# TensorE takes both halves' high products of a weight unit before both halves' low ones

## The chip, the cores and the metric

The kernel runs on one core of a Trainium2 chip. The metric is the device time of one execution in microseconds (us), as the median of several. The engines are TensorE (PE in the rows, its weight loads PEld), VectorE (DVE), ScalarE (ACT), GpSimd (POOL) and SyncE (SP, which here issues the DMAs of the weights). Each runs its own list of instructions in order, and they wait for each other by semaphores.

## The reference

Two transformer blocks work on 256 tokens of width 1024, in float32. The first is an attention layer with compressed, selected and windowed keys. The second has two layers: a mixer (stick-breaking attention beside a short convolution), then a dense feed-forward part in layer 0 and a mixture of experts in layer 1, and a gated projection. Cut to what matters:

```python
for i in range(DEPTH_2):
    ...                                   # h = h + mixed @ w_o[i]
    f = rmsnorm(h, ffn_norm_g[i])
    if i % 2 == 0:
        h = h + swiglu(f, dense_w1[j], dense_w3[j], dense_w2[j])
    else:                                 # top 2 of 8 experts, 1024 -> 3584 -> 1024
        h = h + moe_swiglu(f, router_w[j], moe_w1[j], moe_w3[j], moe_w2[j])
    gate = jax.nn.sigmoid(rmsnorm(h, ple_norm_g[i]) @ ple_gate_w[i])
    h = h + gate * (p[i] @ ple_proj_w[i])
```

## The kernel before

**Three products for one.** A float32 matrix product is made from products of the shorter type fp32r: each operand is split into a high part (the value rounded) and a low part (the rest), and PE adds up high x high and low x high (activations times `wh`, L1471 and L1472) and high x low (`wl`, L1476).

**Weight units.** All weights come in units of 128 partitions x 2048 columns (1 MB; some are smaller): as a rule four k tiles of 512 output columns. SyncE loads unit u into one of 6 buffers `raw` (L466) when DVE has finished with unit u-6 (`low_done`). ACT copies it half by half (two k tiles each) to `whi`, one of 3 buffers (`SPL`, L549), and DVE subtracts to get `wlo` (L892). ACT waits, half by half, for `half_used`: PE has finished with that half of unit u-3. It tells DVE and PE by `high_done`, DVE tells PE and SyncE by `low_done`. Where each of the two stands in its own list with its splits is written out by hand: `split_to(v)` makes all halves up to unit v, and between such calls stand the other steps of the stage.

**Products.** `products` (L1461) does one unit: for each half it waits for `high_done`, takes the high products of its k tiles for all output tiles, waits for `low_done`, takes the low ones, and gives the half back with `half_used`. A callback `middle` runs before the second half. `block` (L1482) does the units of one output block; in the first block after a norm its `middle` is `turn_rows(norm, 1)`, which transposes the second half of the token rows (L1527; the rows of the trace show the helper's line, L1454). ACT scales and copies these to `xh` (L565), DVE makes `xl` (L903), and PE waits for that (`xl_done`, L1492) before the second unit. That happens in four blocks: the first of each mixer and the first of each gated projection. Two more calls have a `middle`: the last unit of the dense part (L1745) and the first after the attention (L1696). `unit_T` (L1698) does units with the weights as the stationary operand (L1716, L1717, L1723), with the same order written out; it stands for the second half of each mixer's input and for most of the dense part. `z_half` (L1584) calls `products` for one half at a time.

**The expert rounds.** 8 rounds (L1937), one for each expert, of 42 units; one output tile of 128 gathered tokens, so that a unit is 12 products. First 7 hidden blocks of 4 units (gate, up), with `turn_hidden` between; ACT makes the activation (L735) and copies the turned hidden block (`mTh`, L726), DVE multiplies (`ht`, L1158) and takes the low part (`mTl`, L1149). Then 14 units of the second weight. After six of them PE gathers the next round's tokens (`gather(1)`, L1928 and L1929), for which it waits for `pick` (L1395): DVE makes it after its subtractions for the two units that come behind the gather (`split_to(ub + 4 * NFB + 5 + AHEAD)`, L1166). ACT and DVE then split the gathered tokens (`xgh`, `xgl`). At the end ACT and DVE split the expert's result (`yh` L864, `yl` L1431), and PE scatters it back to the tokens (L1955, L1956). DVE makes `yl` after its subtractions for the first two units of the next round.

Of the kernel before, what the change touches and what calls it, by code (L numbers as in the profile page):

```python
# [108 lines left out]
def build(nc, t, out):  # L109
# [25 lines left out]
    with ExitStack() as ctx:  # L135
# [1313 lines left out]
        def _(pe):  # L1449
# [6 lines left out]
            def split_view(u, nk, n):  # L1456
                s = u % SPL
                return (whi[:, s, 0:nk * n].rearrange("p (k n) -> p k n", k=nk),
                        wlo[:, s, 0:nk * n].rearrange("p (k n) -> p k n", k=nk))

            def products(u, nk, n, hi, lo, k0, outs, first, last, middle=None, halves=(0, 1)):  # L1461

                wh, wl = split_view(u, nk, n)
                for half in halves:
                    if half and middle:
                        middle()
                    ks = range(half * nk // 2, (half + 1) * nk // 2)
                    pe.wait_ge(high_done, g.at(high_done, 2 * u + half + 1))
                    for k in ks:
                        for T, o in enumerate(outs):  # L1470
                            mm(o, hi(k0 + k, T), wh[:, k, :], start=first and k == 0, stop=False)  # L1471
                            mm(o, lo(k0 + k, T), wh[:, k, :], start=False, stop=False)  # L1472
                    pe.wait_ge(low_done, g.at(low_done, 2 * u + half + 1))
                    for k in ks:
                        for T, o in enumerate(outs):
                            ins = mm(o, hi(k0 + k, T), wl[:, k, :], start=False, stop=last and k == nk - 1)  # L1476
                    ins.then_inc(half_used, 1)
# [4 lines left out]
            def block(u, b, hi, lo, kt=KD, n=NB, nt=NT, units=None, norm=None, between=None):  # L1482


                bank = pair(b)
                outs = [ps[:, bank + T, 0:n] for T in range(nt)]
                start_block(b)
                ku = units or KU
                nu = -(-kt // ku)
                for i in range(nu):  # L1490
                    if norm is not None:
                        pe.wait_ge(xl_done, 2 * norm + i + 1)  # L1492
                    if i and between:
                        between()
                    products(u + i, min(ku, kt - i * ku), n, hi, lo, i * ku, outs, i == 0, i == nu - 1,
                             (lambda: turn_rows(norm, 1)) if norm and i == 0 else None)
# [87 lines left out]
            def z_half(i):  # L1584

                if i % 4 == 0 and i:

                    pe.wait_ge(z_done, i // 4)
                u = i // 2
                products(U["z"] + u, KU, NB, *X, (u % 2) * KU, [ps[:, T, :] for T in range(NT)], u % 2 == 0,  # L1590
                         u % 2 == 1, halves=(i % 2,))
# [94 lines left out]
            for i in range(2):  # L1686
                b = B["nsa_out"] + i
                outs = [ps[:, pair(b) + T, :] for T in range(NT)]
                if i == 0:

                    pe.wait_ge(o_evac, 9)
                for k in range(2):
                    if i == 0:
                        pe.wait_ge(yl_done, k + 1)
                    products(U["nsa_out"] + 2 * i + k, KU, NB, *X, k * KU, outs, k == 0, k == 1,
                             (lambda: turn_y(1)) if i == 0 and k == 0 else None)  # L1696
# [397 lines left out]
```

## Time and profile before

| | us |
|---|---|
| median of 3 runs | 1921.33 (1921.16 to 1925.42) |
| the profiled execution | 1927.16 |
| its span, first to last instruction | 1925.3 |
| PE busy | 1838.6 (95%) |
| DVE busy | 1395.7 (72%) |
| ACT busy | 1220.0 (63%) |
| mean granted clock of PE | 0.974 |

All times below are counted from the span's start. In a row of the timeline stand the start, the length, the engine, the line, the operation, what it writes and reads, how many like it follow each other, and, where the engine stood idle before, for how long and what ended that. Products overlap in PE's pipeline, so the distance from one start to the next is the pace, not the length. A wait for several semaphores is put down to the one that came last by the profile; "issue" is a wait for nothing that it shows.

### The profile page before, as it was taken

What the parts mean: (1) busy time and instruction counts of PE and PEld (TensorE: products, weight loads), DVE (VectorE), ACT (ScalarE), POOL (GpSimd) and SP (SyncE); (2) the same over time, 40 slices, a digit from 0 to 9 for tenths busy, and PEclk for the clock granted to TensorE, in tenths of its full rate; (3) what the DMA queues carried; (4) which work ended last, traced back from release to release, by engine and by line L of the source; (5) the groups of instructions that cost most, each with busy time, mean ns of one, the idle gap of its engine ahead of it and who ended that gap; (6) DMA issues with size and microseconds to landing.
All of it is one profiled execution on the core that took longest, in us unless ns stands there. A gap on an engine that the chain in (4) does not pass through costs nothing.

```text
span 1925.3 us, 26803 instructions
## 1 busy us (share of the span) xinstructions
PE 1838.6 (95%) x9562; PEld 1546.2 (80%) x9562; DVE 1395.7 (72%) x1653; ACT 1220.0 (63%) x1536; POOL 5.9 (0%) x13
## 2 busy tenths in 40 slices
PE   8999979989999989879999999999999999999997
PEld 7877758979998779768878878788788787887885
DVE  4456755746664466458899898898998898989884
ACT  5545544644444455548687777786877777768773
POOL 0000000000000000000000000000000000000000
PEclk9889989999999999879999999999999999999999
DMA  9743223425445344219989899899898998998980
GB/s 321 248 165 109 74 102 131 154 100 190 177 190 202 111 175 176 93 67 339 369 319 362 317 364 364 310 367 355 325 361 319 352 360 325 358 345 343 357 323 23
DMA packets 68336, 483.32 MB, mean 251 GB/s; under 512 B 7610, under 2 KB 7738, under 8 KB 10928
## 3 DMA queue, kind: packets, MB, share of 16 engines
q1 hardware_dynamic: 66480, 475.26, 64.9%
q0 software_dynamic: 1792, 7.18, 1.8%
q8 instruction: 44, 0.72, 0.2%
q14 instruction: 20, 0.16, 0.0%
HBM read 478.22 MB, written 4.19 MB: 251 GB/s over the span
## 4 chain that ended last, share of the span: by engine, by line
PE 80%; DVE 8%; ACT 6%; issue 5%; DMA 0%; ACTq 0%; DVEq 0%; POOLq 0%
PE ps L1471 20%; PE ps L1472 19%; PE ps L1476 19%; DVE wlo L892 4%; PE ps L1716 4%; PE ps L1723 4%; PE ps L1717 4%; PE ps L1454 3%; ACT whi L549 2%; PE ps L1928 1%; PE ps L1929 1%; ACT xgh L846 1%; DVE sg L1015 1%; ACT sg L672 1%; PE ps L1819 1%
## 5 line engine op out<-in xcount | busy, mean ns | idle before, releaser
L892 DVE TENSOR_TENSOR wlo<-raw,whi 128x1024 fp32r<-128x1024 f32 x906 | 1044.1, 1212 | 171.8 <-ACT whi L549 171.3
L549 ACT ACTIVATE whi<-raw 128x1024 fp32r<-128x1024 f32 x906 | 904.2, 1055 | 154.6 <-PE ps L1476 127.4
L1471 PE MATMUL ps<-whi,xgh 128*128 128x512 f32 x896 | 360.2, 402 | 4.6 <-ACT whi L549 4.6
L1472 PE MATMUL ps<-whi,xgl 128*128 128x512 f32 x896 | 355.0, 396 | 0.0
L1476 PE MATMUL ps<-wlo,xgh 128*128 128x512 f32 x896 | 282.2, 396 | 0.0
L1471 PE MATMUL ps<-whi,xh 128*128 128x512 f32 (+1 forms) x448 | 186.9, 418 | 21.9 <-issue 9.9
L1471 PEld LDWEIGHTS ps<-whi,xgh 128*128 128x128 f32 x896 | 168.9, 188 | 43.1 <-ACT whi L549 4.8
L1476 PEld LDWEIGHTS ps<-wlo,xgh 128*128 128x128 f32 x896 | 168.9, 188 | 40.8
L1472 PEld LDWEIGHTS ps<-whi,xgl 128*128 128x128 f32 x896 | 169.2, 189 | 37.8
L1472 PE MATMUL ps<-whi,xl 128*128 128x512 f32 (+1 forms) x448 | 181.3, 406 | 0.0
L1471 PE MATMUL ps<-whi,mTh 128*128 128x512 f32 x448 | 178.3, 398 | 0.0
L1472 PE MATMUL ps<-whi,mTl 128*128 128x512 f32 x448 | 177.1, 395 | 0.0
L1716 PE MATMUL ps<-xh,whi 128*128 128x256 f32 x640 | 157.9, 284 | 0.5 <-DVE xl L903 0.5
L1717 PE MATMUL ps<-xl,whi 128*128 128x256 f32 x640 | 157.0, 283 | 0.0
L1476 PE MATMUL ps<-wlo,mTh 128*128 128x512 f32 x448 | 140.9, 395 | 0.0
L1471 PEld LDWEIGHTS ps<-whi,xh 128*128 128x128 f32 x448 | 90.3, 202 | 43.5 <-issue 20.6
L1476 PE MATMUL ps<-wlo,xh 128*128 128x512 f32 (+1 forms) x448 | 123.8, 401 | 0.0
L1716 PEld LDWEIGHTS ps<-xh,whi 128*128 128x128 f32 x640 | 122.7, 192 | 1.0 <-DVE xl L903 0.7
L1717 PEld LDWEIGHTS ps<-xl,whi 128*128 128x128 f32 x640 | 122.8, 192 | 0.1
L1472 PEld LDWEIGHTS ps<-whi,xl 128*128 128x128 f32 x448 | 90.3, 202 | 17.6 <-issue 0.2
L1476 PEld LDWEIGHTS ps<-wlo,xh 128*128 128x128 f32 x448 | 87.8, 199 | 18.9
L1476 PEld LDWEIGHTS ps<-wlo,mTh 128*128 128x128 f32 x448 | 84.2, 188 | 20.4
(288 smaller groups left out, 1902.5 us busy)
## 6 DMA issues: line engine op xcount, KB each, us to landing
raw<-in_w_moe_dram SPq DMA_DIRECT2D x336, 1024.0 KB, 6.7
raw<-in_w_fixed_dram SPq DMA_DIRECT2D x112, 1024.0 KB, 4.9
bias_scratch<-revb POOLq DMA_DIRECT2D x1, 3072.0 KB, 39.2
bias<-bias_scratch POOLq DMA_DIRECT2D x1, 2048.0 KB, 18.2
raw<-in_w_fixed_dram SPq DMA_DIRECT2D x4, 512.0 KB, 4.2
tok<-in_xt_dram SPq DMA_DIRECT2D x2, 512.0 KB, 4.5
h<-in_x_dram SPq DMA_DIRECT2D x1, 1024.0 KB, 13.6
out_dram<-h SPq DMA_DIRECT2D x2, 512.0 KB, 2.8
```

What stands on the lines that cost most here:

```text
L549: AC(whi[:, v % SPL, c], raw[:, v % RAW, c], ACT.Copy).then_inc(high_done, 1)
L672: ins = AC(sg[:, i % 2, r, 0:nk], sg[:, i % 2, r, 0:nk], ACT.Exp, scale=SC, bias=ast_[:, i, 1, r:r + 1], accum_out=ast_[:, i, 2, r:r + 1])
L846: ins = AC(xgh[:, j, :], ps[:, 6 + j // 4, (j % 4) * P:(j % 4 + 1) * P], ACT.Copy, scale=gains[:, 5, j:j + 1])
L892: V.tensor_tensor(wlo[:, v % SPL, c], raw[:, v % RAW, c], whi[:, v % SPL, c].bitcast(F32), ALU.subtract).then_inc(low_done, 1)
L1015: ins = V.tensor_tensor_reduce(sg[:, i % 2, r, 0:nk], ps[:, bank, (r // 2) * S:(r // 2) * S + nk], bias[:, hh, S - nk:S], 1.0, MASKED, ALU ...
L1454: return nc.tensor.transpose(dst, src, ident if idn is None else idn)
L1471: mm(o, hi(k0 + k, T), wh[:, k, :], start=first and k == 0, stop=False)
L1472: mm(o, lo(k0 + k, T), wh[:, k, :], start=False, stop=False)
L1476: ins = mm(o, hi(k0 + k, T), wl[:, k, :], start=False, stop=last and k == nk - 1)
L1716: mm(o, w_, xh[:, kk, :], start=kk == 0 and c % 2 == 0, stop=False, skip_group_check=True)
L1717: mm(o, w_, xl[:, kk, :], start=False, stop=False, skip_group_check=True)
L1723: ins = mm(o, wl[:, k, c * P:(c + 1) * P], xh[:, kk, :], start=False, stop=kk == KD - 1, skip_group_check=True)
```

## The change

In `products` the loop over the halves is cut in two: first, for each half, the wait for its high part, and its high products (`middle` still comes ahead of the second half); then, for each half, the wait for its low part, its low products and the signal `half_used`. With two halves the order is high 0, (`middle`), high 1, low 0, low 1 in place of high 0, low 0, (`middle`), high 1, low 1. A call for one half does what it did. `unit_T` isn't touched.

```diff
                 for half in halves:
                     if half and middle:
                         middle()
-                    ks = range(half * nk // 2, (half + 1) * nk // 2)
                     pe.wait_ge(high_done, g.at(high_done, 2 * u + half + 1))
-                    for k in ks:
+                    for k in range(half * nk // 2, (half + 1) * nk // 2):
                         for T, o in enumerate(outs):
                             mm(o, hi(k0 + k, T), wh[:, k, :], start=first and k == 0, stop=False)
                             mm(o, lo(k0 + k, T), wh[:, k, :], start=False, stop=False)
+                for half in halves:
                     pe.wait_ge(low_done, g.at(low_done, 2 * u + half + 1))
-                    for k in ks:
+                    for k in range(half * nk // 2, (half + 1) * nk // 2):
                         for T, o in enumerate(outs):
                             ins = mm(o, hi(k0 + k, T), wl[:, k, :], start=False, stop=last and k == nk - 1)
                     ins.then_inc(half_used, 1)
```

## Rows read from the trace of the kernel before

**Rows 1.** The page, part 4: the chain that ended last, by engine.

```profile
PE 80%; DVE 8%; ACT 6%; issue 5%; DMA 0%; ACTq 0%; DVEq 0%; POOLq 0%
```

**Rows 2.** Busy us, expert rounds: length; PE, PEld, DVE, ACT, POOL; clock, DMA share, GB/s.

```profile
857.00:1880.00 1023.00, 1015.58 (x4589) 821.29 (x4590) 890.37 (x909) 774.30 (x887) 0.00 (x0) 1.00 0.89 341
```

**Rows 3.** Waits of PE and PEld, 860 to 1880: total us, times, longest.

```profile
PE ps L1955 <- DVE yl L1431: 6.2, 8, 0.8
...
PEld ps L1955 <- DVE yl L1431: 9.7, 8, 1.2
PEld ps L1928 <- issue: 4.4, 8, 0.6
```

**Rows 4.** Line L892 (DVE's subtractions), whole span: who waited for it (us, times).

```profile
  PEld ps L1723: 0.4, 2
```

**Rows 5.** Timeline of PE: the unit before the last one ahead of the gather.

```profile
1207.61 0.40 PE L1471 MATMUL ps<-whi,mTh 128*128 128x512 f32 x1
...
1208.54 0.63 PE L1476 MATMUL ps<-wlo,mTh 128*128 128x512 f32 x2
...
1210.40 0.40 PE L1471 MATMUL ps<-whi,mTh 128*128 128x512 f32 x1
```

**Rows 6.** Timeline of ACT and DVE in the loop over the hidden blocks.

```profile
1179.72 0.69 DVE L1149 TENSOR_TENSOR mTl<-ps,mTh 128x512 fp32r<-128x512 f32 x1 [0.91 <-ACT mTh L726]
...
1185.81 1.22 DVE L892 TENSOR_TENSOR wlo<-raw,whi 128x1024 fp32r<-128x1024 f32 x1
...
1185.95 1.06 ACT L549 ACTIVATE whi<-raw 128x1024 fp32r<-128x1024 f32 x1 [0.34 <-PE ps L1476]
```

**Rows 7.** Timeline of ACT and DVE ahead of the gather.

```profile
1202.71 4.84 ACT L549 ACTIVATE whi<-raw 128x1024 fp32r<-128x1024 f32 x5
...
1209.20 1.06 ACT L549 ACTIVATE whi<-raw 128x1024 fp32r<-128x1024 f32 x1 [0.34 <-PE ps L1476]
...
1203.79 9.17 DVE L892 TENSOR_TENSOR wlo<-raw,whi 128x1024 fp32r<-128x1024 f32 x8 [0.26 <-ACT whi L549]
1212.88 0.48 DVE L1395 TENSOR_SCALAR pick<-con,slot 128x128 fp32r<-128x128 f32 x2
```

**Rows 8.** Timeline of PE: into the gather, and the first product behind it.

```profile
1212.74 0.63 PE L1476 MATMUL ps<-wlo,mTh 128*128 128x512 f32 x2
1213.49 0.32 PE L1928 MATMUL ps<-pick,xnh 128*128 128x128 f32 x1
...
1217.11 0.45 PE L1471 MATMUL ps<-whi,mTh 128*128 128x512 f32 x1
```

**Rows 9.** Timeline of ACT, DVE and PE at the end of a round.

```profile
1235.56 1.06 ACT L549 ACTIVATE whi<-raw 128x1024 fp32r<-128x1024 f32 x1 [0.34 <-PE ps L1476]
...
1237.49 2.34 DVE L892 TENSOR_TENSOR wlo<-raw,whi 128x1024 fp32r<-128x1024 f32 x2
1239.76 1.31 DVE L1431 TENSOR_TENSOR yl<-ps,yh 128x512 fp32r<-128x512 f32 x2
...
1240.49 0.51 PE L1955 MATMUL ps<-yh,pickT 128*128 128x512 f32 x1 [0.77 <-DVE yl L1431]
```

**Rows 10.** First block of the first gated projection, timeline; then L1471's wait, 0 to 1925.

```profile
664.26 1.07 PE L1476 MATMUL ps<-wlo,xh 128*128 128x512 f32 x4
...
666.25 1.57 ACT L565 ACTIVATE xh<-ps,con 128x256 fp32r<-128x256 f32 x4 [6.20 <-PE ps L1454]
...
667.89 1.07 PE L1476 MATMUL ps<-wlo,xh 128*128 128x512 f32 x4
...
669.56 0.50 PE L1471 MATMUL ps<-whi,xh 128*128 128x512 f32 x1 [0.60 <-DVE xl L903]
...
PE ps L1471 <- DVE xl L903: 6.0, 5, 3.5
```

**Rows 11.** Busy us by stretch, as rows 2: around a wait, and at the last stage's start.

```profile
405.00:415.00 10.00, 8.43 (x42) 6.77 (x41) 5.33 (x8) 3.46 (x6) 0.00 (x0) 1.00 0.12 36
...
1886.00:1892.50 6.50, 4.91 (x12) 3.85 (x13) 1.35 (x4) 0.00 (x0) 0.00 (x0) 0.50 0.00 0
```

## The prediction

> **What bounds the kernel now.** I read the chain that ended last first: TensorE (PE) is 80% of it, most of it weight products [rows 1]. Then the busy times by stage: the expert rounds, from 857 to 1880 us, are over half of the span, and in them PE is busy for 1015.6 of 1023 us at full clock, with VectorE (DVE) at 87% and ScalarE (ACT) at 76% [rows 2]. The waits of that stretch name only two places where PE stands still, each once in every one of the 8 rounds: before the scatter (L1955, 6.2 us of PE idle in all), and before the gather (L1928, where only the weight loads' row shows it, 4.4 us) [rows 3]. No low half of a weight unit ever kept a product of L1476 waiting; the two waits for DVE's subtractions, 0.4 us in all, belong to L1723, which the change doesn't touch [rows 4]. So the wait on `low_done` that the new order puts off is free already. What is left of the change is its timing: when a half is given back, and when `middle` runs.
>
> **The products themselves.** Their number and operands stay. A unit of a round is 12 products, 1207.61 to 1210.40, 0.233 us each, high or low [rows 5]. The new order has the same kinds of neighbours, always another stationary tile, so I take 0 for it.
>
> **What moves: the release of half 0.** `half_used` of half 0 now comes after four more products, 4 x 0.233 = 0.93 us later in a round; half 1 is given back when it was. ACT may split half 0 of unit u+3 only then. In the steady loop over the hidden blocks this is covered. There ACT's split of a first half stands at 1185.95, released by PE; it would start at 1186.88 and end (1.06 us) at 1187.94, while DVE, in arrears, comes to that half two steps of 1.135 us after 1185.81, at 1188.08. That is 0.14 us of cover, and behind it DVE waits 0.91 us for another thing anyway (the turned hidden block, 1179.72 in the rows), which takes up a slip before it adds up [rows 6]. PE had the high halves ready long before. Cost 0.
>
> **Before the gather it is not covered.** Here DVE's list is: eight subtractions, 1203.79 on, then the two `pick` tiles (1212.88), and the gather on PE waits for those. ACT's splits in front of it are released by PE: the one that DVE's last but one subtraction needs starts at 1209.20 [rows 7], 0.03 us after the low products that began at 1208.54 and lasted 0.63 [rows 5]. In the new order these start at 1209.47, so the split starts at 1210.13 and ends at 1211.19. DVE came to this half at 1203.79 + 6 x 1.136 = 1210.61; now it starts at 1211.23, 0.62 us later, and with it the last subtraction and `pick`. PE had stood still there for 0.28 us already (1213.49 where 1213.21 was due after the two products of 1212.74 [rows 8]), so nothing is left to absorb it: 0.62 us per round, 8 rounds, 5.0 us. What is queued behind it on PE is the whole rest of the round, and nothing there gives it back, since ACT's and DVE's next work starts from the gather's end.
>
> **At the end of a round** ACT's split at 1235.56 is released by PE too. It moves to 1236.49 and ends at 1237.55; DVE came to it at 1237.49 and starts at 1237.59, 0.10 us late. Its next subtraction and the low part `yl` (1239.76) follow without a gap, and the scatter's 0.77 us of waiting (1240.49) grows by the same [rows 9]. 8 x 0.10 = 0.8 us.
>
> **What is gained: `middle`.** In the first block after a norm, `middle` turns the second half of the rows (L1527, shown as L1454) between the halves. It now runs before the four low products of half 0 in place of after them. In the block that starts the first gated projection PE's low products start at 664.26, the turns follow, ACT copies them from 666.25, and PE, after its last low products (667.89 + 4 x 0.227 = 668.80), waits until 669.56 for the low part of that copy: 0.76 us from start to start, 0.60 of them idle [rows 10]. With the turns 0.91 us sooner the wait is gone, as ACT and DVE had nothing else to do there (6.20 us idle). L903 ended five waits of L1471, 6.0 us, of which 3.5 are one at the start of the last stage that doesn't move; the other four, 2.5 us, are this place in the four such blocks [rows 10]. With the 0.16 us of overlap each: 2.5 + 4 x 0.16 = 3.1 us. Two of them run partly at half clock, where the turns take longer too; I leave that in the range. The other two uses of `middle` give nothing: at the end of the dense part the next stage waits for DVE's addition after the last product, and after the attention PE doesn't wait.
>
> **Other places with two output tiles** (a unit of 24 products, 5.4 us): the release comes 8 x 0.227 = 1.8 us later, but ACT and DVE need 1.9 and 2.3 us for a unit, so they are done long before the need. PE has no wait for them [rows 4]. The transposed products (L1716 on) and the z blocks, called half by half, keep their order. SyncE's loads wait for `low_done`, which comes up to 0.7 us later there; ACT never waits for a load.
>
> **Sum.** +5.0 + 0.8 - 3.1 = +2.7 us on the profiled execution: span 1925.3 to 1928.0 us. That execution took 1927.16 us, 5.8 above the median of the three timed runs, 1921.33; on the median the forecast is 1924.0 us (+0.14%). A measurement of this kernel can tell about 0.3%, 5.8 us, from no change.
>
> **The clock.** At the granted clock the rounds are at 1.00; the last stage's first block is at 0.50 after its waits (the lower of the two levels, 1.2 GHz), and a standstill of 1.57 us (8.43 of 10 us busy, 405 to 415) leaves the clock at 1.00 [rows 11]. My longest new standstill is 0.28 + 0.62 = 0.90 us, so I expect none of the rounds to fall. The Trainium skill ("TensorE: Matmul & The Clock Gate", Part 1: The HAM clock gate) says that the slow clock is the default and that activity releases it. By that rule a standstill in each round is the risk of this change, and it is rival (f).
>
> If each of the 8 gathers ran its 32 small products at half clock, 3.6 us (1213.49 to 1217.11 [rows 8]) would become 7.2, 8 x 3.6 = 29 us in all; the standstill of 1.57 us speaks against it.
>
> The same page (Back-to-back issue gap) gives about 216 ns for a 512-column product at full clock; the rows have 233. By 216 the shift before the gather would be 0.86 and the loss 0.55 us per round. The trace's 233 decides.
>
> **Rivals.**
> (a) Net small, as summed: 1921 to 1928, 0.60.
> (b) The stall before the gather is hidden after all, because DVE's steps close up or ACT's release isn't the one I take it for. Then only the gain of 3.1 and the 0.8 are left: 1919.0. For it: DVE's arrears cover every other place. Against it: at that half ACT ends at 1209.20 + 1.06 = 1210.26 today and DVE starts at 1210.61, 0.35 us of cover against 0.93 of shift. 0.13.
> (c) Slower than before: the lost lead isn't taken up by DVE's arrears. The full 0.93 us arrives at the gather and, at the end of the round, the 0.48 us by which a second half is late behind a first half that is 0.93 late (splits that wait for nothing start 0.95 us apart [rows 7], those that PE releases 1.40: 0.93 + 0.95 - 1.40). With no gain at the norms: 8 x 1.41 = 11.3 us, 1932.6. It decides from 0.73 us per round on without the gains (5.8 / 8), from 1.11 with them. The hidden loop is the third place that could pay, by six blocks a round, once its 0.14 and 0.91 us are used up. 0.19.
> (d) PE gets a faster pace from the new order. Blocks whose stationary tile is `xh` run at 0.227 us, those of the rounds at 0.233; if the order were the cause, 8 x 42 x 12 = 4,032 products x 0.0067 = 27 us, 1894. Both paces hold alike in high and low products, so I give 0.02.
> (e) The change does nothing that can be seen: ACT always has the halves ready, neither term comes: 1921.3. 0.05.
> (f) The clock falls at each gather, as worked out above: 1924 + 29 = 1953. 0.01.
>
> Range: from (b) less 1.5 us for the clock, 1917.5, to most of (c), 1931. Within 0.3%: (a), (b), (e) nearly whole and the lower part of (c): 0.77. Slower 0.19, faster 0.04 ((d) and chance).
>
> **What would show it.** In the profile after: the wait before L1928 0.62 us longer in each round; ACT's two splits of a unit 0.95 us apart in the rounds in place of 1.40; the first product of the second unit after each norm without a wait for L903; a round 0.7 us longer; a pace of 0.233 us. I am wrong if the rounds keep their length (b), if PE waits in the hidden loop (c), or if the pace moves (d).

## The result, and the profile after

| | before | after |
|---|---|---|
| median, timed side by side | 1924.56 us (1921.16 to 1926.49, 7 runs) | 1929.39 us (1928.51 to 1933.19, 7 runs) |
| ratio after / before | | 1.0032, 95% interval 1.0022 to 1.0042 |
| the profiled execution | 1927.16 us, span 1925.3 | 1928.51 us, span 1926.7 |
| mean granted clock of PE, that execution | 0.974 | 0.972 |

The change costs 0.32% of 1924 us, 6.2 us (the two medians alone are 4.8 us apart; the ratio goes by all fourteen executions). The forecast was +2.7 us, outside the interval of 4.2 to 8.1 us. The median of before is 3.2 us higher in seven runs than in the three that the forecast started from, so the comparison that counts is +2.7 against +6.2. (One later execution of after took 3635 us; it is left out everywhere, and why it did is not known.) The two profiled executions hide most of it: that of before is 2.6 us above its own median, that of after is the fastest of its seven.

First the page of after, part 4 (the chain that ended last, by engine), which answers to [rows 1]:

```profile
PE 82%; DVE 8%; issue 5%; ACT 4%; DMA 0%; DVEq 0%; ACTq 0%; POOLq 0%
```

PE is as dominant as before. Two percent more of the chain is PE and two percent less ACT; I read nothing more into that.

The waits of the expert rounds in after (total us, times, longest), which answer to [rows 3]:

```profile
PEld ps L1955 <- DVE yl L1431: 10.6, 8, 1.3
PEld ps L1928 <- issue: 9.4, 8, 1.2
PE ps L1955 <- DVE yl L1431: 7.0, 8, 0.9
...
PE ps L1928 <- DVE pick L1395: 6.0, 8, 0.7
```

Before the gather the weight loads' wait has gone from 4.4 us to 9.4 (0.55 to 1.18 a round), and PE now has a row of its own there, 6.0 us, which it hadn't. Before the scatter PE waits 7.0 us in place of 6.2. No other line of PE appears for the rounds: the loop over the hidden blocks stayed covered.

How it comes about shows in the timeline of ACT and DVE ahead of the gather in after, then that of PE; they answer to [rows 7, 8]:

```profile
1204.66 2.01 ACT L549 ACTIVATE whi<-raw 128x1024 fp32r<-128x1024 f32 x2 [0.74 <-PE ps L1476]
1207.46 2.01 ACT L549 ACTIVATE whi<-raw 128x1024 fp32r<-128x1024 f32 x2 [0.79 <-PE ps L1476]
...
1208.56 2.36 DVE L892 TENSOR_TENSOR wlo<-raw,whi 128x1024 fp32r<-128x1024 f32 x2 [0.44 <-ACT whi L549]
1210.83 0.48 DVE L1395 TENSOR_SCALAR pick<-con,slot 128x128 fp32r<-128x128 f32 x2
```

```profile
1209.60 1.10 PE L1476 MATMUL ps<-wlo,mTh 128*128 128x512 f32 x4
1211.44 0.32 PE L1928 MATMUL ps<-pick,xnh 128*128 128x128 f32 x1 [0.74 <-DVE pick L1395]
```

ACT's two splits of a unit now follow each other (one row of two, 2.01 us), where PE used to release them one at a time. The first of the last pair starts at 1207.46 and is done about 1.06 us later, and DVE, which ran through without a gap before, stands still for 0.44 us for it. `pick` comes late by that much and more, and PE by 0.62 us: 0.74 where it was 0.12. In the rows of three successive gathers of after the distance is one round:

```profile
1083.06 0.32 PE L1928 MATMUL ps<-pick,xnh 128*128 128x128 f32 x1 [0.75 <-DVE pick L1395]
...
1211.44 0.32 PE L1928 MATMUL ps<-pick,xnh 128*128 128x128 f32 x1 [0.74 <-DVE pick L1395]
...
1339.80 0.32 PE L1928 MATMUL ps<-pick,xnh 128*128 128x128 f32 x1 [0.75 <-DVE pick L1395]
```

It is 128.38 and 128.36 us; in the trace of before a round is 127.66. (By a round's length I mean, here and below, the distance between such starts of successive rounds. The first round, which begins at the lower clock, is longer by 2.2 to 2.5 us in every kernel here, with or without the change.) So each round is 0.72 us longer: 0.62 at the gather and 0.10 at the scatter, where PE waits 0.88 in place of 0.77. 8 x 0.72 = 5.8 us.

At the norms, in the first block of the first gated projection, the low products of the first unit run on into the second unit in after; this answers to [rows 10]. The row below them is the wait for `xl` that is left in the whole span.

```profile
662.45 1.99 PE L1476 MATMUL ps<-wlo,xh 128*128 128x512 f32 x8
664.28 0.39 PE L1470 MATMUL ps<-whi,xh 128*128 128x512 f32 x1
...
PE ps L1470 <- DVE xl L903: 3.5, 1, 3.5
```

L903 ended five waits of 6.0 us; it ends one of 3.5. The 2.5 us of waits are gone, as forecast; the 0.64 us of overlap that the forecast added to them have no row of their own.

Waits alone would give 5.8 - 3.1 = +2.7 us, which is the forecast and is not what was measured. The rest must be in something that isn't a wait, and two stretches point to the granted clock (busy us by stretch, as in [rows 2]: length; PE, PEld, DVE, ACT, POOL; clock, DMA share, GB/s). After:

```profile
857.00:1884.00 1027.00, 1012.55 (x4584) 818.49 (x4583) 891.82 (x910) 763.78 (x885) 0.00 (x0) 1.00 0.90 340
1892.50:1895.00 2.50, 2.50 (x11) 2.20 (x11) 0.00 (x0) 0.00 (x0) 0.00 (x0) 0.50 0.00 0
```

Before:

```profile
1892.80:1895.50 2.70, 2.70 (x17) 2.33 (x16) 0.00 (x0) 1.56 (x5) 0.00 (x0) 0.99 0.00 0
```

In this trace of after the rounds keep the full clock, as forecast. But the last stage, which had its clock back by 1892.8, is still at the lower level (1.2 GHz) up to 1895.0, with 11 products in 2.5 us against 17 in 2.7. The mean clock of the seven executions of after is 0.9721 on average; that of before is 0.9747 to 0.9751 on average in the sets of executions below. One part of clock in a thousand is one thousandth of the span's products, 1.9 us at most, if PE is busy all that time. So my theory for the experiments was that the waits are as forecast and that the rest, some 3.5 us, is time at the lower clock, at places that one trace need not show.

### The profile page after: what moved, and what is told of

It reads as the page before. It is cut to its first block, busy times and chain, and to the rows that moved or that the text cites. A ratio compares the mean times of both kernels' runs of the same rounds, so it can differ in the third digit from the quotient of the medians.

```text
span 1926.7 us, 26803 instructions
## 1 busy us (share of the span) xinstructions
PE 1838.4 (95%) x9562; PEld 1547.5 (80%) x9562; DVE 1396.1 (72%) x1653; ACT 1209.0 (63%) x1536; POOL 5.9 (0%) x13
## 4 chain that ended last, share of the span: by engine, by line
PE 82%; DVE 8%; issue 5%; ACT 4%; DMA 0%; DVEq 0%; ACTq 0%; POOLq 0%
PE ps L1470 20%; PE ps L1471 20%; PE ps L1476 20%; PE ps L1716 4%; PE ps L1723 4%; PE ps L1717 4%; DVE wlo L892 4%; PE ps L1454 3%; ACT whi L549 1%; PE ps L1928 1%; PE ps L1929 1%; DVE sg L1015 1%; ACT sg L672 1%; PE ps L1819 1%; PE ps L1538 1%
## 5 line engine op out<-in xcount | busy, mean ns | idle before, releaser
L892 DVE TENSOR_TENSOR wlo<-raw,whi 128x1024 fp32r<-128x1024 f32 x906 | 1044.9, 1213 | 178.1 <-ACT whi L549 173.4
L549 ACT ACTIVATE whi<-raw 128x1024 fp32r<-128x1024 f32 x906 | 893.0, 1050 | 204.3 <-PE ps L1476 182.5
L1471 PE MATMUL ps<-whi,xgl 128*128 128x512 f32 x896 | 354.9, 396 | 0.0
L1476 PE MATMUL ps<-wlo,xgh 128*128 128x512 f32 x896 | 246.1, 396 | 0.0
L1471 PEld LDWEIGHTS ps<-whi,xgl 128*128 128x128 f32 x896 | 169.2, 189 | 37.9
L1471 PE MATMUL ps<-whi,xl 128*128 128x512 f32 (+1 forms) x448 | 183.0, 410 | 0.0
L1471 PE MATMUL ps<-whi,mTl 128*128 128x512 f32 x448 | 177.0, 395 | 0.0
L1476 PE MATMUL ps<-wlo,mTh 128*128 128x512 f32 x448 | 122.9, 396 | 0.0
L1476 PE MATMUL ps<-wlo,xh 128*128 128x512 f32 (+1 forms) x448 | 113.0, 391 | 0.0
L1471 PEld LDWEIGHTS ps<-whi,xl 128*128 128x128 f32 x448 | 91.6, 204 | 18.1 <-issue 0.2
L1470 PEld LDWEIGHTS ps<-whi,mTh 128*128 128x128 f32 x448 | 84.1, 188 | 19.8
```

Of the source, the lines that this page charges most:

```text
L549: AC(whi[:, v % SPL, c], raw[:, v % RAW, c], ACT.Copy).then_inc(high_done, 1)
L892: V.tensor_tensor(wlo[:, v % SPL, c], raw[:, v % RAW, c], whi[:, v % SPL, c].bitcast(F32), ALU.subtract).then_inc(low_done, 1)
```

## The experiments

Every kernel was timed in five rounds beside before. Ratios are to before, with 95% intervals. In the diffs `new` says where the changed order is used; elsewhere the old one stands.

**Which part of the program pays.** One kernel has the new order in the rounds alone, one everywhere else alone.

```diff
+                new = (g.r is not None and not g.post)        # rounds only
+                new = not (g.r is not None and not g.post)    # outside only
```

> The new order only in the expert rounds, the old one everywhere else. My theory (half 0 is given back later, and DVE's list in front of the pick and of yl has no cover for it): each round is 0.72 us longer, 8 x 0.72 = +5.8 us over the kernel before; the wait before L1928 goes from 0.12 to 0.75 us, the one before L1955 from 0.77 to 0.87; the waits for L903 stay as before. The rival that the products themselves run at another pace in the new order: the pace leaves 0.233 us. The rival that the change's cost lies outside the rounds (the measured ratio of 1.0032 is some 3 us more than the +2.7 that I summed up): this kernel shows less than +3 us.

> The new order everywhere but in the expert rounds. My theory: the rounds are as before (127.7 us each), the four blocks after a norm lose their wait for L903, 3.1 us less than before. The rival that the cost beyond my sum lies outside the rounds: no gain, or up to 3 us more than before, with the time in stages at half clock.

Measured: rounds only 1930.5 us, ratio 1.0044 (1.0030 to 1.0058); outside only 1922.91 us, ratio 1.0002 (0.9993 to 1.0011). All of the loss comes from the rounds, and the part outside, with its four waits gone, brings nothing that can be measured. The trace of the rounds-only kernel has rounds of 128.36 to 128.40 us, but two of 131.5. Three stretches of it, one ahead of a gather and two behind one (columns as above):

```profile
1334.00:1341.00 7.00, 6.26 (x36) 5.10 (x35) 4.50 (x6) 2.31 (x3) 0.00 (x0) 1.00 0.96 363
1341.60:1348.40 6.80, 6.80 (x24) 5.74 (x23) 2.51 (x9) 4.41 (x11) 0.00 (x0) 0.52 0.39 165
1601.00:1607.80 6.80, 6.80 (x26) 5.93 (x26) 1.57 (x7) 3.78 (x10) 0.00 (x0) 0.52 0.48 194
```

And the timeline of PE through the first of them:

```profile
1339.07 0.32 PE L1947 MATMUL ps<-pick,xnh 128*128 128x128 f32 x1 [0.74 <-DVE pick L1395]
...
1341.57 0.28 PE L1947 MATMUL ps<-pick,xnh 128*128 128x128 f32 x1
1341.68 0.28 PE L1948 MATMUL ps<-pick,xnl 128*128 128x128 f32 x1
...
1342.16 0.41 PE L1947 MATMUL ps<-pick,xnh 128*128 128x128 f32 x1
1342.37 0.41 PE L1948 MATMUL ps<-pick,xnl 128*128 128x128 f32 x1
...
1344.40 0.63 PE L1470 MATMUL ps<-whi,mTh 128*128 128x512 f32 x1
1344.83 0.63 PE L1471 MATMUL ps<-whi,mTl 128*128 128x512 f32 x1
...
1348.91 0.40 PE L1471 MATMUL ps<-whi,mTl 128*128 128x512 f32 x1
1349.14 0.40 PE L1470 MATMUL ps<-whi,mTh 128*128 128x512 f32 x1
```

PE stood still for 0.74 us, then ran its small products 0.11 us apart, and in the midst of them, 2.7 us after the standstill, the distance doubles to 0.21; the next unit's products are 0.43 us apart in place of 0.23, and after 6.8 us the clock is back. This costs the round 3.1 us. This is what was missing: the clock does fall in some rounds, though not in all of them as rival (f) had it. ("Fall" stands below for such a stretch in a round.)

**Is it the release ahead of the gather?** The new order everywhere but in the six units ahead of the gather.

```diff
+                new = not ((g.r is not None and not g.post)
+                           and U["ffn1"] + 4 * NFB <= u < U["ffn1"] + 4 * NFB + 6)
```

> The changed kernel, with the old order in the six units of each round that stand ahead of the gather. My theory: ACT gets half 0 of the unit that DVE needs for its last but one subtraction 0.93 us sooner again, so the wait before L1928 is 0.12 us as before, while the 0.10 us at the scatter and the gain after the norms stay: 5.0 us less than the changed kernel, 2.3 less than before by my terms. The rival that the gather's wait has another source (the pick itself, or DVE falling behind over the whole round): the wait stays at 0.75 us.

Measured: 1922.56 us, ratio 0.9994 (0.9985 to 1.0003). Rounds of 127.74 us, 0.08 over before: the scatter's term. The waits of PE in its rounds:

```profile
PE ps L1974 <- DVE yl L1431: 7.0, 8, 0.9
```

The scatter's wait is that of after, the gather's isn't there, and no stretch of its rounds is at the lower clock. Six units of 42 carry the whole wait of a round but 0.1 us. (That a single trace shows no fall says little; the trace of after has none either.)

**The release alone, and more of it.** The old order of the products, but in the rounds both halves are given back at the unit's end.

```diff
-                    ins.then_inc(half_used, 1)
+                    if g.r is None or g.post:
+                        ins.then_inc(half_used, 1)
+                    elif half:
+                        ins.then_inc(half_used, 2)
```

> The old order of products, but in the rounds both halves are given back together at the unit's end: half 0 is 6 products, 1.40 us, later than before (0.93 in the change). Only the release moves, no product. My theory, by the same steps: before the gather ACT's split starts at 1210.60 in place of 1209.20, DVE's subtraction at 1211.70 in place of 1210.61, so +1.09 us per round; at the end of the round +0.57; in the loop over the hidden blocks DVE slips by 0.37 us in each block, which its wait of 0.91 us for the turned block takes up, 0. Together 8 x 1.66 = +13.3 us. If the hidden loop's cover doesn't hold, it is 6 x 0.37 us more in each round, +31 us. If the change's cost came from the order of the products and not from the release: 0.

Measured: 1945.59 us, ratio 1.0122 (1.0106 to 1.0137), 22 us more than before. In its trace a round is 129.30 us, +1.64 where 1.66 was expected; 8 of them make 13.1. Two stretches that begin in the gathers of the first two rounds are at the lower clock:

```profile
957.00:963.00 6.00, 6.00 (x24) 5.42 (x24) 0.30 (x2) 2.51 (x9) 0.00 (x0) 0.50 0.54 221
1089.00:1096.00 7.00, 7.00 (x29) 6.22 (x29) 1.42 (x6) 3.62 (x10) 0.00 (x0) 0.55 0.53 217
```

with a third from 1868.0 us on, in the last gather. The waits of PE:

```profile
PE ps L1931 <- DVE pick L1395: 9.7, 8, 1.2
PE ps L1958 <- DVE yl L1431: 9.4, 7, 1.3
```

So the delay of a release by a known time moved the gather by what the two lists of ACT and DVE say, without any change of the order in which PE multiplies: the late release alone is enough for the loss. 13.1 us of waits and three falls of 3.1 are 22.4 us.

**The same again, and the part outside by itself.** To see how much one trace or one set of runs can say, after and before were each run once more as if they were new kernels; a third kernel has the old order with only `middle` put ahead of the low products of half 0.

```diff
-                    if half and middle:
-                        middle()
...
+                    if middle and not half:
+                        middle()
                     pe.wait_ge(low_done, g.at(low_done, 2 * u + half + 1))
```

> The changed kernel once more, for a second trace of it and more timed executions. The theory after the first four runs: each round is 128.38 us by the release alone, and on top the clock can fall to half for 6.8 us just behind the standstill at a gather, at 3.1 us a time. Then this trace has rounds of 128.4 us and, if one is longer, it is by 3.1 us and holds a stretch at half clock that begins in its gather; the median is 5 to 8 us over before. The rival: all that lies between my +2.7 and the measured +6 is in stages outside the rounds; then all rounds are 128.4 us in every trace of it and e1's two long rounds are an accident of that kernel.

> The kernel before, unchanged, for a second trace of it (the first one's execution was 4 us above the median of its kind). Ratio 1.000. No round holds a stretch at half clock, since its standstill at the gather is 0.12 us; all rounds 127.66 us. Outside the rounds it has less time at half clock than e2's trace (109 us), some 90 to 95 us, since its mean granted clock is 0.976 in most executions against 0.973 in e2's. If rounds of this kernel fall to half clock too, the clock is no part of what the change costs.

> The kernel before, with middle (the turn of the second half of the rows) moved ahead of the low products of half 0 and nothing else: high 0, middle, low 0, high 1, low 1. The release of half 0 is only as much later as middle takes. By my prediction's term the four waits for L903 vanish: 3.1 us less than before. By what e2 measured (no gain, and a lower mean clock): the waits vanish, but the kernel isn't faster by more than 1 us, since the turns at half clock and the shift of the stretches at half clock give the time back.

Measured: after 1931.58 us, ratio 1.0034 (1.0021 to 1.0047), as the first time; before 1923.97 us, ratio 0.9999 (0.9990 to 1.0008); `middle` alone 1922.38 us, ratio 0.9995 (0.9984 to 1.0007), an interval that just reaches the forecast of -3.1 us. In the second trace of after one round of eight is 131.53 us long, with this stretch behind its gather:

```profile
1342.00:1348.80 6.80, 6.80 (x27) 5.93 (x26) 1.51 (x6) 3.72 (x10) 0.00 (x0) 0.52 0.30 127
```

The second trace of before has no such round. For `middle`, two stretches show where part of its gain went: the start of the second mixer's output block, where no `middle` runs, and the first block of the last stage, where one does. The second trace of before:

```profile
779.00:789.00 10.00, 10.00 (x43) 8.26 (x44) 5.51 (x7) 9.91 (x12) 0.00 (x0) 0.83 0.29 105
1877.00:1889.00 12.00, 8.41 (x33) 6.75 (x34) 1.66 (x4) 2.46 (x7) 0.00 (x0) 0.72 0.00 0
```

`middle` alone:

```profile
779.00:789.00 10.00, 10.00 (x37) 8.26 (x37) 5.48 (x7) 9.91 (x12) 0.00 (x0) 0.66 0.32 105
1877.00:1889.00 12.00, 6.84 (x24) 5.56 (x25) 3.23 (x7) 1.57 (x4) 0.00 (x0) 0.57 0.00 0
```

The four waits for L903 are gone here too. But the mean clock of the first stretch is 0.66 in place of 0.83, and that of the second 0.57 in place of 0.72: in all 1.7 us and 1.8 us of full-speed time less in 22 us. Over all executions the mean clock was 0.9730, against 0.9748 of before in the same set, about 3.4 us.

The fourteen traces of this document agree with it. Add up PE's time at the lower clock from 265 us to the rounds and in the last stage, up to the last 10 us of the span: it is 68.3 us in each of the seven traces with the old place of `middle`, and 71.7 to 82.0 us, 75.6 on average, in the seven with the early one. Ahead of 265 us the averages are 27.3 and 27.8. The 7.3 us more, at half speed, are 3.6 us of products. The stages themselves say the same: from the first rows turned in the first mixer (282.65 us in the trace of before) to those turned at 822.17, and from those of the last stage (1882.96) to the end, the seven with the old place take 581.5 us on average and the seven with the early one 581.4. The mixer of layer 1 is even longer by 1.3 us in five of them. So nearly all that the saved waits give is taken back by more time at the lower clock, in part at places where nothing was saved. Why the clock comes back later there I can't say from the traces.

**A cure for the gather.** After's order, but DVE makes `pick` one unit of subtractions sooner, ahead of the last two instead of behind them.

```diff
-                split_to(ub + 4 * NFB + 5 + AHEAD)
-                extra()
+                split_to(ub + 4 * NFB + 4 + AHEAD)
+                pick_first()
+                split_to(ub + 4 * NFB + 5 + AHEAD)
+                extra()
```

> The changed kernel, with pick made by DVE one unit of subtractions sooner (behind those of the first unit that follows the gather, not the second). The release of half 0 stays late. My theory: pick is ready before PE comes to the gather, PE's 0.75 us of standing still and the 0.16 us of overlap before it go, 0.9 us per round, and with the standstill the falls of the clock in the gather go too: rounds of 127.5 us, 7 us less than the changed kernel's undisturbed rounds, at or a little under the kernel before. If the falls of the clock come from the gather's small products and not from the standstill, single rounds are still 3.1 us longer.

Measured: 1919.31 us, ratio 0.9979 (0.9968 to 0.9991). A round is 127.33 us, 1.0 less than in after and 0.3 less than in before; no round of its trace has the lower clock. The waits of PE in the rounds:

```profile
PE ps L1954 <- DVE yl L1430: 7.0, 8, 0.9
```

With the changed order of products untouched and the wait for `pick` gone, the kernel is faster than both. The loss of the rounds is at that one wait, but for the scatter's 0.1 us.

**Only the standstill.** In the slower kernels so far the release of the halves and PE's standstill change together. Here before's own order and releases stand, and DVE does one more subtraction ahead of each `pick`.

```diff
                     dve.wait_ge(pick_turned, g.at(pick_turned, n))
+                    step(V.tensor_tensor(yl[:, :NB], h[:, 0, :NB], h[:, 1, :NB], ALU.subtract))
```

> The kernel before with its own order of products and its own releases; the one difference is that VectorE, ahead of picking each next round's tokens, does one more 128x512 subtraction of h into yl, which is not in use then (about 0.67 us by the like operation of L1431), and waits for its end. So TensorE finds nothing to do for about 0.7 us longer at each gather, as in the changed kernel, but nothing else of the order or of the weight units is touched. Theory (the standstill behind the small products alone lets the clock fall): undisturbed rounds of 127.6 + 0.7 = 128.3 us, TensorE's wait for pick 0.75 to 0.85 us in all 8 rounds, and in a trace 0 to 3 of the 8 rounds 3.1 us longer, each with 6.8 us at half clock that begin in or just behind the gather; median 5.6 us over before from the waits plus about one to two falls of 3.1 us: +7 to +12 us, ratio 1.0036 to 1.0062. Rival (the falls come from the order of the products, by which high products follow one another for 7.4 us, and not from the standstill): the same waits but no round with a fall, +5.6 us, ratio 1.0029.

Measured: 1935.87 us, ratio 1.0060 (1.0047 to 1.0073). Undisturbed rounds are 128.23 us, +0.57, less than the 0.7 expected, and 8 x 0.57 = 4.6 us is less than half of what was lost. The gather's waits, and the stretch behind the first gather:

```profile
PE ps L1929 <- DVE pick L1396: 6.0, 8, 0.9
```

```profile
960.50:967.50 7.00, 7.00 (x28) 6.31 (x28) 1.00 (x4) 3.20 (x10) 0.00 (x0) 0.53 0.49 204
```

A second such stretch, of 6.8 us too, begins in the last gather, at 1862.0 us. The mean clock of its six executions is 0.9705 against 0.9747 of before, some 8 us. So a standstill of 0.7 to 0.95 us at this place brings the falls, with the old order of products and the old releases; the rival, that the order does it, is out: its ratio of 1.0029 lies below the interval. (Its "7.4 us" was wrong besides: in a round the eight high products of a unit take 8 x 0.233 = 1.9 us.)

**The standstill filled.** The same kernel, with three products that nobody needs just ahead of PE's wait.

```diff
+                if n:
+                    for _ in range(3):
+                        mm(ps[:, 7, :], xnh[:, 0, :P], xnh[:, 0, :NB], start=True, stop=True)
                 pe.wait_ge(pick_done, g.at(pick_done, n + 1))
```

> The kernel of the late pick (before's order, VectorE's extra 0.67 us ahead of each pick), and with it three products of 128x512 on TensorE just ahead of its wait for pick, into a buffer that the gather overwrites; nobody waits for them. They take 3 x 0.233 = 0.70 us of the 0.95 us for which TensorE stood still there. The rounds should end as late as in the late pick without them (128.25 us, +0.6 each, 4.8 us in all), since pick comes no sooner. Theory (TensorE's standstill at the gather lets the clock fall in some rounds, some 8 us of the 12.9 us by which the late pick was slower): no fall in any round, mean clock back at 0.974 to 0.976, +4.8 us on before, ratio 1.002 to 1.003. Rival (what the late pick lost beyond its waits comes from something else, as a round that begins later against its transfers): ratio 1.005 to 1.007 as without the three products, clock 0.970.

Measured: 1931.0 us (1925.22 to 1931.04, 5 runs), ratio 1.0037 (1.0024 to 1.0051). The timeline of PE in one round, and the busy times of all rounds:

```profile
1208.48 0.85 PE L1923 MATMUL ps<-xnh 128*128 128x512 f32 x3
1209.37 0.32 PE L1932 MATMUL ps<-pick,xnh 128*128 128x128 f32 x1
```

```profile
857.00:1885.00 1028.00, 1016.95 (x4610) 822.39 (x4608) 894.62 (x919) 773.04 (x888) 0.00 (x0) 1.00 0.88 339
```

The gather comes as late as without the three products (rounds of 128.23 us), there is no fall in the rounds of its trace, and the mean clock of its five executions is back at 0.9744 (before 0.9748). Eight gathers without a fall would alone say little, as after's first trace has none either; the mean clock, 0.9705 without the three products, is what supports the theory. The time agrees less well: the forecast ratio of 1.002 to 1.003 is at the lower end of the interval, the rival's 1.005 to 1.007 just reaches its upper end, and three of the five executions are 5 us above the other two at a mean clock that differs by 0.001, which is worth 2 us. The clock is back; some 2 us of this kernel's time are not explained.

**A version that beats both.** Before's order, with `middle` ahead of the low products of half 0, `pick` one unit sooner, and each half of `yl` made between the halves of DVE's last subtractions; and the same with `middle` in its old place.

```diff
-                split_to(ub + UNITS_ROUND - 1 + AHEAD)
+                split_to(ub + UNITS_ROUND - 2 + AHEAD)
+                split_half(0)
+                yl_half(0)
+                split_half(1)
+                yl_half(1)
```

> The order of before in all units (high, low, high, low), but with the norm block's middle() put ahead of the low products of half 0; VectorE picks the next round's tokens one unit of subtractions sooner (as in the run with the early pick), and takes each half of yl between the two halves of the last unit's subtractions. Gather: the wait of 0.12 us goes and with it the small products' other waits, 127.65 to 127.35 us as the early pick gave it with the new order. Scatter: PE's wait of 0.77 us at L1955 falls by the time for which yl waited behind the last subtractions; how much is open, since ACT's yh may then be what is late: 0.1 to 0.5 us. Theory: rounds of 126.8 to 127.2 us, so -3.5 to -6.8 us from 8 rounds, and 0 to -3.1 us from middle() of which the clock gave nearly all back in the run of it alone: -3.5 to -8 us, ratio 0.9958 to 0.9982. Rival (yh is late in any case): the scatter wait stays at 0.77 us, rounds at 127.35, -2.4 us, ratio 0.9987.

> The kernel of the run beside this one with middle() back in its old place, behind the low products of half 0. Theory (what middle() saves in waits is given back by more time at half clock): the same time as the run beside it within 1.5 us, though four waits of 3.5 us in all for L903 are back. Rival (the gain is real and was only hidden by the luck of few executions): 3 us above the run beside it.

Measured: 1915.37 us, ratio 0.9962 (0.9949 to 0.9976), and with the old `middle` 1916.56 us, ratio 0.9966 (0.9953 to 0.9979). Rounds are 126.98 us in both, 0.68 less than in before. The first kernel's waits in the rounds:

```profile
PE ps L1962 <- DVE yl L1182: 3.9, 8, 0.5
```

The scatter's wait has fallen from 0.77 us to 0.49. The last `yl` now starts at 1233.55, within 0.1 us of the ends of both ACT's `yh` (0.60 us from 1232.91) and DVE's own subtraction, so a still earlier place in DVE's list would win nothing. The two kernels differ by 1.2 us where the waits say 3.1; the early `middle` has a mean clock of 0.9732, the old one 0.9744, about 2.3 us. That is the third pair with a lower clock for the early `middle`, and again the difference of time is within what the intervals allow for none.

**The account.** Of all kernels: the waits by the traces (8 rounds at the round's difference to 127.66, and -3.1 us for an early `middle`), the mean clock of all executions against that of before in the same set, times 1925 us, their sum, and what was measured (ratio less one, times 1923 us).

| kernel | waits, us | clock | x 1925, us | sum | measured |
|---|---|---|---|---|---|
| after again | 5.8 - 3.1 | 0.9716 / 0.9748 | 6.2 | +8.9 | +6.5 |
| rounds only | 5.8 | 0.9732 / 0.9751 | 3.6 | +9.4 | +8.5 |
| outside only | -3.1 | 0.9728 / 0.9751 | 4.4 | +1.3 | +0.4 |
| old ahead of gather | 0.6 - 3.1 | 0.9735 / 0.9751 | 3.0 | +0.5 | -1.2 |
| late release | 13.1 | 0.9695 / 0.9751 | 10.8 | +23.9 | +23.5 |
| `middle` alone | -3.1 | 0.9730 / 0.9748 | 3.4 | +0.3 | -1.0 |
| early pick | -2.6 - 3.1 | 0.9730 / 0.9748 | 3.4 | -2.3 | -4.0 |
| late pick | 4.6 | 0.9705 / 0.9747 | 8.1 | +12.7 | +11.5 |
| late pick, filled | 4.6 | 0.9744 / 0.9748 | 0.7 | +5.3 | +7.1 |
| both, early `middle` | -5.4 - 3.1 | 0.9732 / 0.9747 | 3.0 | -5.5 | -7.3 |
| both, old `middle` | -5.4 | 0.9744 / 0.9747 | 0.6 | -4.8 | -6.5 |

The sums follow the measurements within 2.4 us over a spread of 31. They are mostly 1 to 2 us too high, as one would expect where some of the time at the lower clock is idle for PE: 1925 us times the difference is an upper bound, and the eleven fit best with 1.6 us per 0.001 in place of 1.9. (Over the 74 executions of before beside them, 0.001 of clock goes with 1.1 us, at clocks given to 0.001 only.) Without the clock's column four of the eleven would be off by 3.5 to 10.4 us.

## Why the prediction was right and wrong

**Right, by its own steps.** The pace is 0.233 us per product in the new order too (1204.93 to 1205.16 and on in the trace of after), so rival (d) is out. The loop over the hidden blocks stayed covered; even the release of the run with both halves late, 1.40 us of delay, left it so, and (c), which needed the lead to be lost there or in full at the gather, didn't come. The gather's term was forecast at 0.62 us and measured at 0.62 (0.12 to 0.74), the scatter's at 0.10 and measured at 0.10 (0.77 to 0.88); together 0.72 us a round, as the rows of after show. (PE had stood idle for 0.12 us there; the prediction's 0.28 us counted 0.16 us of overlap between products too, and its 0.90 us of standstill was 0.74.) The four waits after the norms are gone. ACT's two splits of a unit follow each other at once. (b) and (e) are out with the rounds' length.

**Wrong: the clock in the rounds.** The step that failed is "My longest new standstill is 0.28 + 0.62 = 0.90 us, so I expect none of the rounds to fall". I took it from one stretch, which holds a standstill of 1.57 us that left the clock alone [rows 11]. This is its row:

```profile
410.24 1.09 PE L1454 MATMUL ps<-con,h 128*128 128x128 f32 x8 [1.57 <-DVE h L1271]
```

The same stands at 822.17. Behind it come 8 small products, 0.85 us, and then wide ones of 512 columns. The one at the gather is half as long but is followed by 32 small products, 3.6 us, and there the clock does fall: in 0, 1, 2, 3 and 2 rounds in the traces of after, after again, rounds only, late release and late pick, 8 times in 40 gathers, always 1.7 to 2.7 us behind the end of the wait. In the nine traces in which the wait is 0.12 us, filled, or gone, it never does, in 72 gathers (one of them waits for 0.3 us). Nor does it ever fall at the scatter, where PE waits for 0.2 to 1.35 us in every round of all fourteen traces, with products of 512 columns behind it. That the small products have a part in it is my reading of these places; no run changed them. What decides in which rounds the clock falls is open too. Rival (f) had the mechanism at 0.01, but priced it as all eight gathers at half clock, 29 us. What the runs show is a fall in some rounds only, at about 3.1 us each: in all 3.6 us by the mean clock of the rounds-only kernel. The Trainium skill ("TensorE: Matmul & The Clock Gate", Part 1: The HAM clock gate) says that the slow clock is what the engine has unless activity holds the fast one. The traces agree, with 0.74 us of idle and the fall 2.7 us behind its end, but they also have 1.57 us of idle without a fall.

**Mis-sized: the gain at the norms.** The term of -3.1 us was right as a sum of waits and wrong as time. By the table, 3 to 4 us of clock go against it wherever `middle` runs early, and outside only, `middle` alone and the pair of the last experiment measured +0.4, -1.0 and -0.8 us in place of -3.1 (the first interval excludes -3.1, the second just doesn't); the stages of the fourteen traces give 0.1 us. The prediction had noticed that two of the four places run partly at half clock and left that to the range; it should have been asked there whether the clock would come back at the same time if the wait were gone.

**The sum, corrected:** 5.8 us of waits in the rounds, about 3.6 us of falls, and -3.1 at the norms with some 2 to 3 us given back: +8 to +9, and 1 to 2 less for the idle part, against 6.2 and 6.5 measured. The time lies inside the range by luck: (c), another mechanism, had set its upper end, and the clock's part was not in it.

## What to carry to other kernels

To move a release by a known time, go through each consumer's list and take the slack of the one instruction that stands before the next wait of the bottleneck engine; that arithmetic gave 0.72 and 1.66 us a round where 0.72 and 1.64 were measured. Then ask of each new standstill of TensorE what it does right behind it: at the gather, with small products behind it, a wait of 0.7 to 1.2 us cost 3 us more in one round of five, and waits saved after the norms gave almost nothing. Products that nobody needs, put into a standstill, kept the mean clock; better is to take what the wait is for out of the queue behind which it stands, as the early `pick` does.

## What the runs showed of the hardware

- The clock fell to its lower level (1.2 of 2.4 GHz) 2.7 us behind the end of a standstill of only 0.74 us (trace of rounds only), in the midst of 32 products of 128 columns, 0.11 us apart. It fell in 8 of the 40 gathers with a wait of 0.7 to 1.2 us ahead of them, and not in the others with the same rows: rounds of 131.5 against 128.4 us. A standstill of 1.57 us with 8 small products and then wide ones behind it left it at 1.00, and so did the scatter's of 0.2 to 1.35 us ahead of wide ones, 112 times in the fourteen traces.
- Each such stretch was 6.8 us long, in four kernels, and lengthened its round by 3.1 to 3.2 us (2.9 and 2.6 in the late pick, where the scatter's wait behind it was 0.22 us in place of 0.78); products of 512 columns went from 0.23 to 0.43 us, those of 128 from 0.11 to 0.21.
- The mean granted clock of a kernel's executions accounts for what its waits don't: taken at 1.9 us per 0.001 it brings eleven kernels, over a spread of 31 us, to within 2.4 us of their measured difference.
